# Two halves of the shared expert's gate and up products computed during routing, the first in chunks inside TensorE's waits

## The chip, the cores and the metric

One Trainium2 chip, of which the kernel uses one core. The metric is the device time of one execution in microseconds (us), from the first to the last instruction with what lies around it. TensorE is called PE, VectorE DVE, ScalarE ACT, GpSimd POOL and SyncE SP, as in the profile; L1384 is line 1384 of the kernel.

## The reference, cut to what matters

Two layers over 272 tokens (16 meta tokens and 256 of the sequence) of width 1024, all in 32-bit floats. Each layer is a mixer, a layer norm, and a mixture of experts: 64 routed experts, of which each token takes 8, and one shared expert that every token takes.

```
scores = sigmoid(h @ w_router); biased = scores + router_bias
# group-limited top 8 of 64 -> gates
act    = silu(h @ w_gate[e]) * (h @ w_up[e]);  routed += gate * (act @ w_down[e])
shared = (silu(h @ sh_gate) * (h @ sh_up)) @ sh_down       # sh_gate, sh_up: 1024 x 256
h      = layer_norm(ALPHA * h + routed + shared)
```

The shared expert's gate and up products together have 512 output columns. Turned over (weights standing still, 272 or 256 tokens streaming), these are four **halves** of 128 rows each: j = 0 and 1 are the gate, j = 2 and 3 the up product. Each half is a sum over 8 chunks of the width, one product (a call of `pe.matmul`) per chunk. A product of 32-bit floats shows as two MATMUL records in the trace, so a half is 16 records.

## The kernel before, in words

The engines run their own instruction lists and meet through semaphores. A stage is a block; at the end of a block all engines meet before the next block begins.

**Routing** (`norm_and_route`, one block per layer). It normalises the mixer's output (`hN`), computes the router's logits and picks experts on DVE in a long chain of small instructions. PE does short pieces between: transposes of the rows for the table in device memory (`turn_rows`, L1587), counts of tokens by expert (`rank_ps`, L1597), a transpose of the selection and the gates (`both_ps`, L1603), the broadcast of two units' places (`spread_unit`, L1421 and L1422), and two products that sort the experts by load (L1612, L1616 to L1618). Between them PE waits for DVE and ACT, and there it multiplies the identity with a constant (`stay_busy(n)`, L1570: n products of 128 rows and 256 columns into bank 4, whose result nobody reads). After the sort, PE waits for the shared gate and up weights (`gu_ready`) and computes as many halves as `halves_ahead(layer)` says: one, j = 0, into bank 6. ACT then takes its SiLU (`shared_silu`, L1393), and with that the block ends. The queue SP issues, in this block, the loads of the shared weights (in layer 1; in layer 0 they are asked for earlier) and, once the order of the experts is known (`ordered`), the load of the fifth expert (L1239 the gate and up matrix, L1258 the down matrix). POOL writes the rows to device memory and issues the first two gathers of rows (L1470).

**Experts** (`experts`, one block per layer). The 64 experts are processed in 27 units of two or four experts (units 2, 7, 12, 17 and 26 have four). Six slots hold expert weights, 3 MB each; SP refills a slot as soon as PE has done with its matrices, by semaphores that PE raises after half of the gate and up products (`gu_low`), after all of them (`gu`) and after the down products (`dn`). For unit i PE runs the gate and up products (L1893), turns the next unit's gathered rows over (`turn`, L1872), combines the unit before (L1911 or L1913), and runs the down products (L1948) into banks `y0b` and `y1b` (banks 4 and 5). ACT and DVE copy these banks out (`ye0`, `ye1`; L2032 and L2116).

After the down products of unit 2 (`SHARED_UNIT`) PE computes the halves of the shared expert that routing left over, j = 1 to 3, with j = 1 in bank 7 and j = 2 and 3 in banks 4 and 5. Before j = 2 it waits for both copies of the down products:

```
for j in range(ahead, 2 * FC):
    if j == FC:
        pe.wait_ge(ye0, i + 1)
        pe.wait_ge(ye1, i + 1)
    shared_half(pe, mem, ex, hN, sh_ps[j], j)
```

Then the slot with the shared gate and up weights (`SHARED_SLOT`) is given to an expert. The first two instructions of the experts block on PE are `turn(0)` and `broadcast(2)`.

Of the kernel before, what the change touches and what calls it, by code (L numbers as in the profile page):

```python
# [25 lines left out]
DC = D // P  # L26
# [1259 lines left out]
def shared_weights(mem):  # L1286
    ring = mem["dense"]
    return ring[:, 0], ring[:, 1].rearrange("p c n -> p (c n)")[:, 0:FC * D].rearrange("p (c n) -> p c n", c=FC)
# [83 lines left out]
def halves_ahead(layer):  # L1372


    return 1


def shared_half(pe, mem, ex, hN, bank, j, cs=range(DC)):


    q, m = divmod(j, FC)
    W, w_gu = hN.shape[-1], shared_weights(mem)[0]
    for c in cs:
        mm = pe.matmul(bank[:, 0:W], w_gu[:, c, q * FF + m * P:q * FF + (m + 1) * P], hN[:, c, :],  # L1384
                       start=(c == 0), stop=(c == DC - 1))
    if cs[-1] == DC - 1:
        mm.then_inc(ex["sh_gu"], 1)
# [28 lines left out]
def spread_unit(pe, mem, ex, i, banks, W):  # L1416


    pe.wait_ge(ex["unit_selected"], i + 1)
    selw, pg = ex["selw"][:, i % AHEAD, :], mem["pg"]  # L1420
    pe.matmul(banks[0][:, 0:W], selw[0:E], pg[0:E, 0:W], start=True, stop=True)  # L1421
    pe.matmul(banks[1][:, 0:W], selw[E:], pg[E:, 0:W], start=True, stop=True).then_inc(ex["rows_broadcast"], 1)  # L1422
# [53 lines left out]
def norm_and_route(nc, k, mem, layer, ex):  # L1476
# [4 lines left out]
    hN, ident, pg, ones, ln, eps = mem["hT"][:, :, first:], mem["ident"], mem["pg"], mem["ones"], mem["ln_par"], mem["eps"]  # L1481
    with ExitStack() as inner:
# [5 lines left out]
        sh_ps = [bank[b] for b in (6, 4, 5, 3)]  # L1488
# [22 lines left out]
        key_off, number, ranks, twice, extras = (sort[:, a:b] for a, b in (  # L1511
            (0, 1), (1, 2), (2, 2 + E), (2 + E, 2 + E + P), (2 + E + P, 2 + 2 * E + P)))
        ahead, warm = halves_ahead(layer), sb("warm", [1, 1])
        loaded, gu_ready = mem["router_loaded"], mem["shared_gate_up_ready"]
        meaned, centred, squared, sq_summed, sd_ready, rooted, scaled, out = (sem(n) for n in (
            "meaned", "centred", "squared", "sq_summed", "deviation", "rooted", "scaled", "normed"))
# [10 lines left out]
        with nc.Block(no_gpsimd_drain=True) as block:  # L1527

            @block.sync
            def _(sp):  # L1530
                if layer > 0:
                    load_shared_gate_up(sp, k, mem, layer)
                load_shared_down(sp, k, mem, layer)
                sp.wait_ge(asked, 1)
                sp.wait_ge(ordered, 1)
                load_expert(sp, k, mem, layer, FIXED)
# [16 lines left out]
            @block.tensor  # L1553
            def _(pe):
                pe.wait_ge(loaded, 48 * (layer + 1))
                for c in range(DC):
                    mm = pe.matmul(bias_ps[0:E, 0:1], wr[:, c, :], shift(c), start=(c == 0), stop=(c == DC - 1))
                mm.then_inc(biased, 1)
                for c in range(DC):
                    pe.wait_ge(squared, c + 1)  # L1560
                    mm = pe.matmul(sqs[:, 0:W], ones[:], sq[:, c, :], start=(c == 0), stop=(c == DC - 1))
                mm.then_inc(sq_summed, 1)
                pe.wait_ge(weighed, 1)
                for c in range(DC):
                    pe.matmul(lg_ps[0:E, 0:W], wg[:, c, :], hN[:, c, :], start=(c == 0), stop=(c == DC - 1)).then_inc(logits, 1)

                def stay_busy(n):

                    for _ in range(n):
                        pe.matmul(bank[4][:, 0:2 * P], ident[:], steady, start=True, stop=True)  # L1570

                stay_busy(2)
                pe.wait_ge(scored, 1)
                for tt, (t0, n) in enumerate(tiles):
                    mm = pe.transpose(sc_ps[0:n, tt * E:(tt + 1) * E], lgT[:, t0:t0 + n], ident[0:E, 0:E])
                mm.then_inc(score_turned, 1)

                def turn_rows(i):
                    half, tt = divmod(i, NT)
                    t0, n = tiles[tt]  # L1580
                    pe.wait_ge(out, 4 * half + 4)
                    if i == 3:
                        pe.wait_ge(bias_in, 1)
                    elif i >= 4:
                        pe.wait_ge(rows_c, i - 3)
                    for c in range(4):
                        mm = pe.transpose(row_ps[i][0:n, c * P:(c + 1) * P], hN[:, 4 * half + c, t0:t0 + n], ident[:])  # L1587
                    mm.then_inc(rows_t, 1)

                for i in range(2 * NT):  # L1590
                    if i == NT:
                        stay_busy(1)
                    turn_rows(i)
                stay_busy(2)
                pe.wait_ge(selected, 1)
                for tt, (t0, n) in enumerate(tiles):
                    mm = pe.matmul(rank_ps[0:E, t0:W], sel[0:n, tt, :], after[0:n, tt, t0:W],  # L1597
                                   start=(tt == 0), stop=(tt == NT - 1))
                mm.then_inc(ranked, 1)
                pe.wait_ge(gated, 1)  # L1600
                pe.wait_ge(rows_c, 3)
                for tt, (t0, n) in enumerate(tiles):
                    mm = pe.transpose(both_ps[:, t0:t0 + n], sg2[0:n, tt].rearrange("p q e -> p (q e)"), ident[0:n, 0:n])  # L1603
                mm.then_inc(ranked, 1)
                stay_busy(2)
                pe.wait_ge(placed, 2)
                pe.wait_ge(rows_c, 2 * NT)
                for i in range(2):
                    spread_unit(pe, mem, ex, i, spread_ps[i], W)
                pe.wait_ge(mem["expert_consts"], 16 * len(EXPERT_CONSTS))  # L1610
                pe.wait_ge(keyed, 1)
                pe.matmul(key_ps[0:E, 0:E], ones[0:E, 0:E], keys[:], start=True, stop=True).then_inc(spread, 1)  # L1612
                stay_busy(1)
                pe.wait_ge(masked, 1)
                pe.wait_ge(placed_by, 2)
                pe.matmul(sort_ps[:, 2 * E:2 * E + 1], twice, rank[:], start=True, stop=True)  # L1616
                pe.matmul(sort_ps[0:1, 0:E], number, at_rank[:], start=True, stop=True)
                pe.matmul(sort_ps[0:1, E:2 * E], cm[:], at_rank[:], start=True, stop=True).then_inc(sorted_, 1)  # L1618
                pe.wait_ge(gu_ready, 32 * (layer + 1))
                for j in range(ahead):  # L1620
                    shared_half(pe, mem, ex, hN, sh_ps[j], j)

            @block.scalar
# [134 lines left out]
def experts(nc, k, mem, layer, ex, out=None):  # L1758
# [11 lines left out]
    with ExitStack() as inner:  # L1770
# [18 lines left out]


        sh_ps, ahead = (None, bank[7], y0b, y1b), halves_ahead(layer)

        spread_to = lambda i: (y0b, y1b) if i < AHEAD else (t0b, t1b)
# [1248 lines left out]
```

## Time and profile before

| | us |
|---|---|
| median of 3 runs | 1540.65 |
| lowest and highest run | 1538.27, 1550.08 |
| the profiled execution, its own time | 1538.58 |
| its span, first to last instruction | 1536.8 |
| PE busy (share of the span) | 1441.6 (94%) |
| DVE busy | 643.1 (42%) |
| ACT busy | 342.2 (22%) |
| hardware_dynamic DMA queue | 481.75 MB, 79.2% of 16 engines' span |
| read from device memory | 508.85 MB |

The page cuts the span into 40 slices of 38.4 us. Layer 0's routing lies around 380 to 405 us and its experts from there to about 890 us; layer 1's routing lies at 1016 to 1042 us and its experts from there to the end. In the slices of the experts the mean busy share of the 16 DMA engines is shown as 9 (90% or more) and the rate as 417 to 426 GB/s; PE is shown as 9 in nearly all of them. A busy PE here is also one that streams 32-bit floats, so PE's busy time alone doesn't say which of the two is the bound.

### The profile page before, as it was taken

To read this page: it belongs to the slowest core of one execution; us is meant where nothing else is said; L and a number is where in the kernel's file an instruction comes from. 1 tells how busy PE (TensorE), PEld (TensorE's weight loads), DVE (VectorE), ACT (ScalarE), POOL (GpSimd) and SP (SyncE) were. 2 spreads that over 40 slices of the span, in tenths; PEclk is the share of its full clock that TensorE was granted. 3 is DMA by queue.
4 is the path that set the end of the run, shared out by engine and by line. 5 is a ranking of instruction groups with operands and counts; after the bars stand their busy time and mean duration, and the time that the engine had idled before them with its cause. 6 is when DMAs were issued, how large, how long until landed. Compare 5 with 4: busy or idle time off the path is not lost. (4 is left out here: it accounts for less than half of the span.)

```text
span 1536.8 us, 24364 instructions
## 1 busy us (share of the span) xinstructions
PE 1441.6 (94%) x9446; PEld 851.0 (55%) x9446; DVE 643.1 (42%) x1451; ACT 342.2 (22%) x714; POOL 249.2 (16%) x331
## 2 busy tenths in 40 slices
PE   8999998999999999896999989999999989979996
PEld 6888768887455545352545467864543433424442
DVE  2766558532533434241433359053233333414334
ACT  3756454310410111110111030141011111101111
POOL 5789625300100000000000000011000000000000
PEclk9999999899999999998999979999999989989998
DMA  8669562058599999999999973499999999999994
GB/s 284 219 189 234 179 167 64 2 215 334 226 417 424 422 419 425 424 422 422 421 424 422 409 287 123 179 387 372 419 424 421 423 424 422 426 421 423 422 422 177
DMA packets 105680, 512.38 MB, mean 333 GB/s; under 512 B 36932, under 2 KB 42116, under 8 KB 68444
## 3 DMA queue, kind: packets, MB, share of 16 engines
q1 hardware_dynamic: 95740, 481.75, 79.2%
q0 software_dynamic: 9824, 29.05, 5.1%
q8 instruction: 78, 1.28, 0.3%
q14 instruction: 38, 0.31, 0.1%
HBM read 508.85 MB, written 17.10 MB: 342 GB/s over the span
## 5 line engine op out<-in xcount | busy, mean ns | idle before, releaser
L1893 PE MATMUL banks<-upper,e_xgT 128*64 128x512 f32 (+1 forms) x880 | 195.5, 611 | 1.8 <-DMA upper<-in_moe_gate_up 1.2
L2102 DVE TENSOR_TENSOR e_ac<-e_sl,banks 128x256 f32<-128x256 f32 x54 | 22.8, 421 | 406.2 <-ACT e_sl L2020 406.2
L366 PE MATMUL banks<-hT,dense_ring 128*128 128x272 f32 x768 | 183.3, 397 | 4.9 <-DMA dense_ring<-in_w_in 4.9
L1470 POOL DMA_INDIRECT x_xg<-rows_dram,x_idx x54 | 53.5, 991 | 823.7 <-DVE x_idx L1462 803.3
L1893 PE MATMUL banks<-dense_ring,e_xgT 128*64 128x512 f32 (+1 forms) x288 | 136.1, 628 | 34.7 <-issue 34.7
L366 PEld LDWEIGHTS banks<-hT,dense_ring 128*128 128x128 f32 x768 | 146.1, 192 | 38.4 <-DMA dense_ring<-in_w_in 5.2
L1893 PE MATMUL banks<-experts,e_xgT 128*64 128x512 f32 (+1 forms) x720 | 160.4, 608 | 1.5 <-DMA experts<-in_moe_gate_up 1.2
L2020 ACT ACTIVATE e_sl<-banks 128x256 f32<-128x256 f32 x54 | 20.7, 384 | 491.6 <-PE banks L1893 491.6
L1893 PEld LDWEIGHTS banks<-upper,e_xgT 128*64 128x64 f32 (+1 forms) x880 | 65.0, 131 | 89.5 <-issue 89.5
L1913 PE MATMUL banks<-x_sg,route_consts 128*128 128x272 f32 x432 | 104.4, 393 | 0.5 <-DVE acc L2089 0.5
L1911 PE MATMUL banks<-route_consts,x_sg 128*128 128x512 f32 x216 | 97.6, 594 | 0.8 <-DVE acc L2086 0.8
L1893 PEld LDWEIGHTS banks<-dense_ring,e_xgT 128*64 128x64 f32 (+1 forms) x288 | 37.9, 133 | 103.1 <-issue 103.1
L1893 PEld LDWEIGHTS banks<-experts,e_xgT 128*64 128x64 f32 (+1 forms) x720 | 53.1, 131 | 75.0 <-issue 75.0
L2069 DVE TENSOR_TENSOR acc<-acc,banks 128x272 f32<-128x272 f32 x208 | 89.5, 438 | 6.4 <-PE banks L1913 3.4
L2116 DVE COPY route_consts<-banks 128x512 f32<-128x512 f32 x54 | 37.4, 692 | 127.4 <-PE banks L1948 127.4
L1913 PEld LDWEIGHTS banks<-x_sg,route_consts 128*128 128x128 f32 x432 | 79.9, 190 | 17.4 <-issue 1.7
L1948 PE MATMUL banks<-experts,e_aT 128*64 128x512 f32 (+1 forms) x360 | 80.2, 596 | 5.1 <-DVE acc L2074 4.8
L1948 PE MATMUL banks<-dense_ring,e_aT 128*64 128x512 f32 (+1 forms) x304 | 80.0, 595 | 3.6 <-DVE acc L2074 3.0
L1948 PE MATMUL banks<-upper,e_aT 128*64 128x512 f32 (+1 forms) x360 | 80.2, 596 | 1.2 <-DVE acc L2069 1.2
L2074 DVE TENSOR_TENSOR acc<-acc,banks 128x512 f32<-128x512 f32 x100 | 68.7, 688 | 22.4 <-PE banks L1911 20.0
L1893 PE MATMUL banks<-x_gate_up,e_xgT 128*64 128x512 f32 (+1 forms) x160 | 75.1, 625 | 0.0
L1872 PEld LDWEIGHTS banks<-ident,x_xg 128*128 128x128 f32 x432 | 46.2, 141 | 46.1 <-issue 43.7
(452 smaller groups left out, 2061.2 us busy)
## 6 DMA issues: line engine op xcount, KB each, us to landing
upper<-in_moe_gate_up SPq DMA_DIRECT2D x45, 2048.0 KB, 26.9
experts<-in_moe_gate_up SPq DMA_DIRECT2D x36, 2048.0 KB, 27.7
upper<-in_moe_down SPq DMA_DIRECT2D x43, 1024.0 KB, 26.2
experts<-in_moe_down SPq DMA_DIRECT2D x43, 1024.0 KB, 26.5
dense_ring<-in_moe_down SPq DMA_DIRECT2D x38, 1024.0 KB, 25.7
dense_ring<-in_moe_gate_up SPq DMA_DIRECT2D x18, 2048.0 KB, 19.8
dense_ring<-in_w_in SPq DMA_DIRECT2D x47, 512.0 KB, 5.4
upper<-in_moe_gate_up SPq DMA_DIRECT2D x20, 1024.0 KB, 14.5
```

The lines of the kernel that those rows point to most:

```text
L366: mm = pe.matmul(ps[g % 4][:, 0:T], slot[:, n % SLOTS_IN, c, :], hT[:, c, :], start=(c == 0), stop=(c == DC - 1))
L1470: pool.indirect_dma_start(out=ex["xg"][:, i % 2, :], out_offset=None, in_=mem["rows_dram"], in_offset=bass.IndirectOffsetOnAxis(ap=ex["idx ...
L1872: mm = pe.transpose((t0b, t1b)[c // 4][:, (c % 4) * P:(c % 4 + 1) * P], xg[:, i % 2, c * P:(c + 1) * P], ident[:])
L1893: mm = pe.matmul(gub[e * n:(e + 1) * n, :], xgT[:, i % 2, c, e * n:(e + 1) * n], gate_up_weights(mem, j)[:, c, :], start=(c == 0), stop=(c ...
L1911: pe.matmul(cb[m][:], sg[:, i % 4, tokens], ys[:, columns], start=True, stop=True).then_inc(cmm, 1)
L1913: pe.matmul(cb[m % 4][:, 0:W], ys[:, m * P:(m + 1) * P], sg[:, i % 4, :], start=True, stop=True).then_inc(cmm, 1)
L1948: mm = pe.matmul(yb[e * n:(e + 1) * n, :], aT[:, f, e * n:(e + 1) * n], down_weights(mem, j)[:, f, h * BLOCK:(h + 1) * BLOCK], start=(f == ...
L2020: act.activation(sl[:], gub[:, 0:FF], ACT.Silu).then_inc(sil, 1)
L2069: dve.tensor_tensor(acc[:, m, 0:W], acc[:, m, 0:W], cb[m % 4][:, 0:W], ALU.add).then_inc(addd, 1)
L2074: dve.tensor_tensor(total[:, tile, columns], total[:, tile, columns], cb[m][:], ALU.add).then_inc(addd, 1)
L2102: dve.tensor_tensor(ac[:], sl[:], gub[:, FF:], ALU.mult).then_inc(mul, 1)
L2116: dve.tensor_copy(ys[:, BLOCK:], y1b[:]).then_inc(ye1, 1)
```

## The change

`halves_ahead` returns 2. Half j = 0 is computed in chunks that stand in four places of PE's list in routing. In layer 0 these are 2, 2 and 1 chunks where identity products stood, and 3 after the sort; in layer 1 the first place keeps its identity products, and the others are 2 and 1 chunks, and 5 after the sort. Half j = 1 follows whole after them, in bank 4. The wait for the shared weights (`gu_ready`) and one for the normalised rows (`out`) stand ahead of each set of chunks. In the experts block `ahead` is 2 as well: after unit 2 only j = 2 and 3 are left, ACT's SiLU of m = 1 moves to routing, and the wait for `ye0` and `ye1` now stands ahead of the first half that is left. Of the eight identity products that `stay_busy` issues in each layer's list, layer 0 keeps three (2 and 1), layer 1 five.

```diff
 def halves_ahead(layer):
-    return 1
+    return 2
...
-                stay_busy(2)
+
+                def shared_chunks(cs):
+                    pe.wait_ge(gu_ready, 32 * (layer + 1))
+                    pe.wait_ge(out, DC)
+                    shared_half(pe, mem, ex, hN, sh_ps[0], 0, cs)
+
+                if layer == 0:
+                    shared_chunks(range(0, 2))
+                else:
+                    stay_busy(2)
                 pe.wait_ge(selected, 1)
...
                 mm.then_inc(ranked, 1)
-                stay_busy(2)
+                in_waits = 2 if layer == 0 else 0
+                shared_chunks(range(in_waits, in_waits + 2))
                 pe.wait_ge(placed, 2)
...
                 pe.matmul(key_ps[0:E, 0:E], ones[0:E, 0:E], keys[:], start=True, stop=True).then_inc(spread, 1)
-                stay_busy(1)
+                shared_chunks(range(in_waits + 2, in_waits + 3))
                 pe.wait_ge(masked, 1)
...
-                pe.wait_ge(gu_ready, 32 * (layer + 1))
-                for j in range(ahead):
+                shared_chunks(range(in_waits + 3, DC))
+                for j in range(1, ahead):
                     shared_half(pe, mem, ex, hN, sh_ps[j], j)
```

## Rows read from the trace of the kernel before

**Rows 1.** Busy by stretch: PE, PEld, DVE, ACT, POOL; PEclk, DMA share, GB/s.

```profile
411.00:415.00 4.00, 4.00 (x22) 1.65 (x19) 0.00 (x0) 0.38 (x1) 0.00 (x0) 1.00 0.95 372
415.00:500.00 85.00, 83.74 (x445) 46.09 (x444) 30.25 (x74) 10.11 (x23) 3.95 (x4) 1.00 1.01 421
...
1051.00:1508.00 457.00, 431.72 (x2066) 179.77 (x2062) 148.81 (x304) 56.89 (x129) 23.64 (x24) 0.98 1.01 421
```

**Rows 2.** Timeline of PE in the experts: start, us, instruction, idle before and releaser.

```profile
720.65 1.03 PE L1893 MATMUL banks<-dense_ring,e_xgT 128*32 128x512 f32 x1 [11.56 <-issue]
...
874.36 3.64 PE L1893 MATMUL banks<-upper,e_xgT 128*32 128x512 f32 x32 [1.21 <-DMA upper<-in_moe_gate_up]
...
1509.53 3.64 PE L1893 MATMUL banks<-experts,e_xgT 128*32 128x512 f32 x32 [1.18 <-DMA experts<-in_moe_gate_up]
```

**Rows 3.** Timeline of routing's end and unit 0, layer 0: PE, ACT.

```profile
394.71 1.13 PE L1597 MATMUL banks<-route_consts,r_sel_gates 128*64 128x272 f32 x6 [0.35 <-DVE r_sel_gates L1714]
...
396.82 1.13 PE L1570 MATMUL banks<-route_consts,ident 128*128 128x256 f32 x4
...
397.88 0.18 PEld L1421 LDWEIGHTS banks<-places_gates,x_selw 64*128 64x128 f32 x1 [0.33 <-DVE places_gates L1727]
...
404.64 0.40 ACT L1393 ACTIVATE shared_act<-banks 128x272 f32<-128x272 f32 x1 [3.84 <-PE banks L1384]
...
405.55 1.07 PE L1872 MATMUL banks<-ident,x_xg 128*128 128x128 f32 x8 [0.94 <-PEq L1527]
```

**Rows 4.** The same timeline in layer 1.

```profile
1033.74 1.03 PE L1570 MATMUL banks<-route_consts,ident 128*128 128x256 f32 x4
...
1037.54 3.72 PE L1384 MATMUL banks<-hT,dense_ring 128*128 128x256 f32 x16
...
1041.29 0.38 ACT L1393 ACTIVATE shared_act<-banks 128x256 f32<-128x256 f32 x1 [3.63 <-PE banks L1384]
...
1043.23 1.09 PE L1872 MATMUL banks<-ident,x_xg 128*128 128x128 f32 x8 [1.97 <-DMA x_xg<-rows_dram,x_idx]
```

**Rows 5.** Timeline after unit 2: PE and DVE, layer 0; PE, layer 1.

```profile
453.44 11.27 PE L1384 MATMUL banks<-hT,dense_ring 128*128 128x272 f32 x48
453.56 0.69 DVE L2116 COPY route_consts<-banks 128x512 f32<-128x512 f32 x1 [2.02 <-PE banks L1948]
...
1091.15 10.63 PE L1384 MATMUL banks<-hT,dense_ring 128*128 128x256 f32 x48
```

**Rows 6.** SP's queue, layer 0: issues by time; landing of the one at 403.95.

```profile
403.95 0.36 SPq L1258 DMA_DIRECT2D dense_ring<-in_moe_down  x1
411.32 4.27 SPq L1246 DMA_DIRECT2D upper<-in_moe_gate_up  x4
...
DMA to landing us min/median/max: 10.4/10.4/10.4
```

**Rows 7.** SP's queue, layer 1: issues by time; landing of the one at 1040.45.

```profile
1040.45 0.36 SPq L1258 DMA_DIRECT2D dense_ring<-in_moe_down  x1
1049.04 4.28 SPq L1246 DMA_DIRECT2D experts<-in_moe_gate_up  x4
...
DMA to landing us min/median/max: 10.8/10.8/10.8
```

**Rows 8.** SP's queue: the shared weights of layer 1; landing of both loads.

```profile
1016.97 5.41 SPq L1276 DMA_DIRECT2D dense_ring<-in_sh_up  x1
...
DMA to landing us min/median/max: 13.0/14.3/15.5
```

**Rows 9.** Chain: PE's start behind DVE's copy; four-expert units without and after a wait.

```profile
1044.36 0.70 DVE e_xgT L2055
1045.06 0.14 issue
...
1174.63 7.00 PE banks L1893 x64
...
1262.80 9.82 PE banks L1893 x64
```

## The prediction

> **What bounds the kernel now.** I first read the busy time by stretch. From 415 us on, and in layer 1 from 1051 to 1508 us, the 16 DMA engines are busy all the time (share 1.01) and move 421 GB/s, while PE is busy too but not quite (431.72 of 457.00 us) [rows 1]. Then the timeline of PE inside the experts, to see who waits for whom. PE catches up with the weights at some of the four-expert units and then stands for up to 11.56 us, and the last unit of either layer waits for its weights (1.21 and 1.18 us) [rows 2]. So each experts stage lasts from the first refill of a slot until the last weights have landed, and what counts is whether the stream of weights has holes. PE's time inside it is worth something only where PE is late with freeing a slot while the stream has run dry. The third view is the timeline of routing and SP's queue, because the stream starts from an almost empty state there: the DMA engines have the fifth expert to move and nothing else until PE is half through unit 0.
>
> **Chunks in place of identity products.** Removed: five identity products in layer 0 and three in layer 1, added as many chunks. Both are 128 rows by 128 weights; an identity product streams 256 columns, a chunk 272 in layer 0 and 256 in layer 1. Three halves, 24 products, take 11.27 us in layer 0 and 10.63 us in layer 1 [rows 5], so a chunk costs 0.47 or 0.44 us; two identity products in the same place show 1.13 us with the tail of the last one [rows 3], the same but for 16 columns (0.03 us each). The idle time behind them covers this: PE waits 0.35 us for the selection, and the weight load of the first broadcast waits 0.33 us for the places [rows 3]. I cost it at nothing in both layers; without that cover it would be 5 x 0.03 = 0.15 us. The two semaphores that stand ahead of the chunks are long raised in layer 0. The wait for `out` is covered by the transposes, which already waited for it.
>
> **The wait for the shared weights in layer 1** stands new ahead of the chunks at 1033.74 us [rows 4]. The later of the two loads is issued at 1016.97 and takes 15.5 us, so it lands at 1032.5 [rows 8], 1.2 us ahead of PE. Behind it on PE are queued both broadcasts, the keys and the sort, and for those wait ACT's copies, DVE's places, POOL's gathers and SP's fifth expert. Price today: nothing; later than 1033.7 it costs one for one.
>
> **The end of routing.** After the sort PE has 3 + 8 = 11 products in layer 0 and 5 + 8 = 13 in layer 1, where it had 8. ACT's SiLU still follows the last one, for j = 1 instead of j = 0, and costs the same. In layer 0 that is 3 x 0.47 = 1.4 us more. Nothing covers it: PE's `turn(0)` at 405.55 was released by the meeting of the engines (PEq), 0.51 us after the end of the SiLU at 405.04 [rows 3]. In layer 1 it is 5 x 0.44 = 2.2 us. There the SiLU ended at 1041.67, PE could have gone on at 1042.2, and it waited for the gathered rows until 1043.23 [rows 4], so 1.05 us are covered and 1.15 are not. Sum at the start of unit 0: +1.4 and +1.15 us on PE.
>
> **What that does to the stream.** The first refill after the fifth expert is asked for at 411.32 in layer 0 and 1049.04 in layer 1, when PE is half through unit 0 [rows 6, 7]. It now comes 1.4 and 1.15 us later. What is the stream doing then? The fifth expert's down matrix lands at 403.95 + 10.4 = 414.35, and in layer 1 at 1040.45 + 10.8 = 1051.25 [rows 6, 7]; so it still runs 3.0 and 2.2 us after the next issue, partly because the two share the engines. Bounds: if the tail is long enough, the stream has no hole and the delay costs 0; if not, it costs all 2.55 us. The row of 411 to 415 us is nearest to the question: at 372 GB/s in place of 421 the stream already lacks 4 x 49 / 421 = 0.47 us there [rows 1]. The tail is nearly used up, so I take about two thirds: 0.9 us in layer 0 and 0.7 in layer 1, **+1.6 us** together. Every microsecond of hole moves the last landing by itself, since the engines are full from then on.
>
> **After unit 2.** Half j = 1 is gone: 8 x 0.47 = 3.8 us in layer 0, 8 x 0.44 = 3.5 us in layer 1. What is late next is the pair of copies. They ran under j = 1. Now j = 2 stands first and waits for DVE's copy, which starts 0.12 us after the halves and takes 0.69 [rows 5]; with 0.14 us for the signal, as between a DVE copy and PE elsewhere [rows 9], PE stands 0.95 us. PE gains 2.8 and 2.6 us net. Against its late start it is then 1.4 us early in both layers. Where does this go? Slots come free earlier, but the stream is full [rows 1]; the next four-expert unit with a wait just waits longer [rows 2]. Worth nothing.
>
> **Sum.** Against the profiled execution: 1538.58 + 1.6 = 1540.2 us. The four executions shown are 1538.27, 1538.58, 1540.65 and 1550.08; their middle is 1539.6, one microsecond above the profiled one. I forecast 1539.6 + 1.6 = **1541.2 us**. A measurement of this kernel can tell about 1%, 15 us, from no change, so this is no change by that measure.
>
> **Rival 1, the gain comes through.** If the stream were full only because slots come free just in time, PE's path would count: +1.4 - 2.8 in layer 0 and +1.15 - 2.6 in layer 1, -2.9 us, 1536.7 us. For it: PE is busy for 94% of its time, and the final waits are only 1.2 us. Against it: there are final waits at all, and 11.56 us in the middle. Chance 0.17.
>
> **Rival 2, nothing arrives.** The tail of the fifth expert covers both delays, and the gain is swallowed as well: 1539.6 us. The 3.0 and 2.2 us of overlap speak for it, the 372 GB/s against it. Chance 0.15.
>
> **Rival 3, slower: the shared weights of layer 1 come late.** Loads of the same kind show 13.0 and 15.5 us to land [rows 8]. It decides from 16.7 us on. At 20 us PE would stand for 3.3 us ahead of the broadcasts, the fifth expert would be asked for as much later while the stream is empty, and the time would be 1541.2 + 3.3 = 1544.5. It is fixed by what was queued ahead of it, and that doesn't change. Chance 0.06.
>
> **Rival 4, slower: one more fall of PE's clock.** After a long wait a four-expert unit's gate and up products take 9.82 us instead of 7.00 [rows 9]. If waits grow from place to place, one more such fall could come where PE has no slack, in the last third of a layer: +2.8 us, 1544.0. Against it: every wait that the change adds is under 1 us, and behind those of 0.94 and 1.97 us in routing the products ran at their usual length [rows 3, 4]. The Trainium skill (TensorE: Matmul & The Clock Gate, section HAM oscillation) says that a wait for data between bursts of products can send the clock back to half; the long waits of this trace agree, and by that rule alone the longer waits at four-expert units would cost more. Chance 0.05.
>
> **That it doesn't do what it says** would show as chunks pushed out of the waits, 0.15 us at most by the sizes above; it is inside the forecast.
>
> **How the numbers follow.** Forecast 0.57, rivals 0.17, 0.15, 0.06, 0.05. The forecast's own range is 1539.6 to 1543.2: from no hole on the middle of the executions to a full hole of 2.55 us on their median, 1540.65. For 8 in 10 I go down to 1536.6, which takes in most of rival 1, and up to 1546.5, which takes in rivals 3 and 4 and an execution or two of the slower kind (one of four lay 10 us up). None of the cases reaches 15 us to either side; what is left is scatter and causes that I don't see: faster 0.02, same 0.95, slower 0.03.
>
> **What the changed kernel's profile would show.** L1384 as x4, x4 and x2 records in layer 0's waits, then x22 after the sort; in layer 1 x4, x2 and x26. `turn(0)` 1.4 us later after the sort in layer 0, and no wait for the gathered rows in layer 1. A DMA share well under 0.95 for a microsecond around the first refill. After unit 2, x32 records behind a wait of about 0.95 us on DVE's copy. Longer waits of PE at the units where it waits today, and the last units still waiting for their weights. I am wrong if the last units stop waiting for weights, if the stream shows no hole, or if layer 1's chunks stand behind a wait for their weights.

## The result, and the profile after

Three sets of 21, 12 and 12 executions of the changed kernel have medians of 1548.53, 1543.99 and 1541.82 us. The first is the result: 1.0037 of the kernel before, interval 1.0019 to 1.0055, so 5.7 us more (2.9 to 8.5), within 1%. On the median of before that was given, 1540.65, this is 1546.35 us: outside the forecast's own range, which ended at 1543.2, and 0.15 us inside the wider one, which ended at 1546.5. The second and third sets are the unchanged repeats `e1` and `e11` below: 1.0011 [0.9982, 1.0041] and 1.0001 [0.9982, 1.0021]. Over all 45 executions the mean is 1545.7; over 134 of before it is 1541.9. The difference is 3.8 us with a standard error of 0.8. Against the executions of before taken beside each set, the means differ by 5.7, 2.4 and 0.2 us, which is more scatter between sets than that error allows for.

The profiled execution took 1548.53 us, 9.95 more than that of before, with a span of 1546.7. It is not typical, as will be seen. The page first: PE's busy time and the bytes.

```profile
span 1546.7 us, 24339 instructions
...
PE 1443.3 (93%) x9430; PEld 850.9 (55%) x9430; DVE 645.5 (42%) x1451; ACT 342.5 (22%) x714; POOL 250.1 (16%) x331
...
q1 hardware_dynamic: 95740, 481.75, 78.8%
```

The same work: PE is busy 1.7 us longer over the whole kernel and the queue moves the same 481.75 MB, in a span that is 9.9 us longer. The time is in waits of the stream of weights. Where the stream runs it runs as before [rows 1]; but in layer 0's unit 0 it stands (busy by stretch, columns as in [rows 1]):

```profile
411.00:415.00 4.00, 4.00 (x16) 2.35 (x18) 1.21 (x3) 0.97 (x2) 0.00 (x0) 0.50 0.77 322
415.00:416.00 1.00, 1.00 (x6) 0.33 (x4) 0.56 (x3) 0.00 (x0) 0.00 (x0) 0.50 0.08 25
416.00:417.00 1.00, 1.00 (x6) 0.27 (x4) 0.00 (x0) 0.00 (x0) 0.56 (x1) 0.85 0.00 0
417.00:418.00 1.00, 1.00 (x8) 0.29 (x6) 0.00 (x0) 0.00 (x0) 0.43 (x1) 1.00 0.00 0
...
440.00:870.00 430.00, 408.18 (x2126) 206.21 (x2125) 159.10 (x389) 52.81 (x119) 22.80 (x23) 0.98 1.01 422
```

From 415 to 418 us almost nothing is moved, where before had 421 GB/s (the last three columns are the granted clock, the DMA share and GB/s). PE's granted clock is at 0.50, the lower of its two levels (1.2 GHz), from 411 to 416 us, and at 1.00 again from 417. PE's timeline says why the stream stands:

```profile
393.99 1.08 PE L1384 MATMUL banks<-hT,dense_ring 128*128 128x272 f32 x4
395.38 1.13 PE L1606 MATMUL banks<-route_consts,r_sel_gates 128*64 128x272 f32 x6 [0.31 <-DVE r_sel_gates L1724]
...
397.50 1.19 PE L1384 MATMUL banks<-hT,dense_ring 128*128 128x272 f32 x4
...
399.98 0.72 PE L1384 MATMUL banks<-hT,dense_ring 128*128 128x272 f32 x2
...
401.39 5.31 PE L1384 MATMUL banks<-hT,dense_ring 128*128 128x272 f32 x22
410.84 1.97 PE L1882 MATMUL banks<-ident,x_xg 128*128 128x128 f32 x8 [4.14 <-DMA x_xg<-rows_dram,x_idx]
...
413.95 8.24 PE L1903 MATMUL banks<-upper,e_xgT 128*64 128x512 f32 x32
...
462.01 7.57 PE L1384 MATMUL banks<-hT,dense_ring 128*128 128x272 f32 x32 [0.90 <-DVE route_consts L2126]
...
877.10 8.75 PE L1903 MATMUL banks<-upper,e_xgT 128*32 128x512 f32 x64 [2.32 <-issue]
...
1043.66 1.03 PE L1384 MATMUL banks<-hT,dense_ring 128*128 128x256 f32 x4
...
1047.46 5.88 PE L1384 MATMUL banks<-hT,dense_ring 128*128 128x256 f32 x26
1054.27 1.07 PE L1882 MATMUL banks<-ident,x_xg 128*128 128x128 f32 x8 [0.93 <-PEq L1527]
...
1519.40 3.64 PE L1903 MATMUL banks<-experts,e_xgT 128*32 128x512 f32 x32 [0.48 <-DMA experts<-in_moe_gate_up]
```

The chunks sit in the waits as x4, x4 and x2 records, 1.08, 1.19 and 0.72 us; the identity products in the last two places show 1.13 [rows 3] and 0.70. After the sort come x22 and x26 records. But then PE stands 4.14 us for gathered rows, `turn(0)` runs at half clock (1.97 us for the 1.07 of [rows 3]), and so do the first of the gate and up products: 32 records take 8.24 us, 7.09 in `e1` below, and the refill is asked for when PE is half through them. The gather is POOL's, and SP loads the fifth expert beside it (timelines of POOL, then of SP):

```profile
397.22 0.51 POOL L1546 DMA_DIRECT2D rows_dram<-r_rows_tail  x1 [0.30 <-ACT r_rows_tail L1660]
402.64 1.09 POOL L1470 DMA_INDIRECT x_xg<-rows_dram,x_idx  x1 [4.91 <-DMA rows_dram<-r_rows_tail]
```

```profile
403.51 0.37 SPq L1239 DMA_DIRECT2D upper<-in_moe_gate_up  x1
404.68 0.36 SPq L1258 DMA_DIRECT2D dense_ring<-in_moe_down  x1
418.94 4.29 SPq L1246 DMA_DIRECT2D upper<-in_moe_gate_up  x4
...
1049.22 0.36 SPq L1239 DMA_DIRECT2D x_gate_up<-in_moe_gate_up  x1
...
1060.05 4.28 SPq L1246 DMA_DIRECT2D experts<-in_moe_gate_up  x4
```

POOL wrote the last rows at 397.22 and waited for them to land; its gather follows at 402.64. In before, POOL's timeline has it waiting for the indices alone:

```profile
400.73 1.09 POOL L1470 DMA_INDIRECT x_xg<-rows_dram,x_idx  x1 [3.68 <-DVE x_idx L1462]
```

There the first gather went out 2.05 us ahead of SP's load at 402.78; here it is 0.87 us ahead. It landed 8.2 us after its issue, in before 3.6. So two things may be in the 5.7 us: the later end of PE's products, which was predicted, and a late gather, which was not.

**The yardstick of what follows.** Call F the issue of the fifth expert (L1239) and R that of the first refill (L1246). "Lost" is the time that the stream lacks in the 25 us after F: 25 x (1 - rate / 421.5), with the mean rate of that stretch and the full rate between 421 and 422 [rows 1]. It leaves out how late F itself is. "Rest" is the time from R to the first product of the next mixer (layer 0) or to the end of the span (layer 1). From all 14 profiles:

| kernel profiled | R - F, 0 | lost, 0 | rest, 0 | R - F, 1 | lost, 1 | rest, 1 |
|---|---|---|---|---|---|---|
| before | 8.54 | 2.16 | 483.06 | 9.73 | 2.52 | 487.76 |
| before, again (`e4`) | 8.54 | 2.05 | 482.83 | 8.70 | 1.45 | 487.75 |
| before, asked 2 (`e9`) | 8.63 | 2.22 | 483.90 | 9.07 | 1.87 | 487.92 |
| changed, again (`e1`) | 9.91 | 2.82 | 483.29 | 10.83 | 3.71 | 488.79 |
| changed, asked 2 (`e10`) | 9.92 | 2.82 | 482.31 | 10.65 | 3.17 | 487.27 |
| changed, third (`e11`) | 9.91 | 2.94 | 482.55 | 10.52 | 3.23 | 488.17 |
| changed, late gather in layer 0 | 15.43 | 7.92 | 483.29 | 10.83 | 3.23 | 486.65 |
| chunks only (`e2`) | 9.27 | 2.58 | 483.46 | 8.58 | 1.45 | 487.95 |
| halves only (`e3`) | 12.21 | 5.13 | 482.43 | 12.12 | 4.36 | 486.54 |
| gain only (`e5`), late in layer 1 | 8.54 | 2.16 | 483.58 | 16.39 | 9.16 | 487.09 |
| before, late (`e6`) | 15.94 | 8.45 | 482.91 | 9.35 | 2.88 | 488.30 |
| changed, late (`e7`) | 17.22 | 9.58 | 483.20 | 10.82 | 3.35 | 487.29 |
| chunks, busy (`e8`), late in layer 0 | 15.23 | 8.63 | 484.15 | 8.86 | 1.57 | 487.80 |
| before, landed (`e12`) | 9.33 | 3.77 | 482.80 | 10.62 | 4.18 | 487.11 |

"Rest" is 482.3 to 484.2 and 486.5 to 488.8 whatever the kernel. What a kernel does to the time is in "lost" and ahead of F. Ahead of F there is scatter in what no edit touches: routing of layer 0 starts at 377.6 to 380.1 us (384.2 in e7; its first DVE instruction), and from the first product of the next mixer to the start of layer 1's routing it is 120.9 to 124.4 us. So the time of one profiled execution says little, and its stretches say more.

### The profile page after: what moved, and what is told of

Same layout as the page of the kernel before. It is cut to its first block and busy times, and to the rows that moved or that the text cites. A ratio compares the mean times of both kernels' runs of the same rounds, so it can differ in the third digit from the quotient of the medians.

```text
span 1546.7 us, 24339 instructions
## 1 busy us (share of the span) xinstructions
PE 1443.3 (93%) x9430; PEld 850.9 (55%) x9430; DVE 645.5 (42%) x1451; ACT 342.5 (22%) x714; POOL 250.1 (16%) x331
## 3 DMA queue, kind: packets, MB, share of 16 engines
q1 hardware_dynamic: 95740, 481.75, 78.8%
```

## The experiments

Each gives its ratio to the kernel before with the 95% interval. The theory was that the delay at the first refill is all that counts, the gain after unit 2 nothing, and that the late gather is an accident of single executions; the main rival, that the gain or the chunks move the time.

**e1 and e4, both kernels again.** No edit.

> The changed kernel once more, for its profile and for how its times fall. Theory (the hole in the weights' stream): the first refill of a slot after the fifth expert sets the end of an experts stage, and it depends on PE's start on unit 0. In the profiled execution of the changed kernel layer 0's first gather was issued only 0.87 us ahead of the fifth expert's load (2.05 us before the change) and took 8.2 us to land instead of 3.6; PE stood for 4.14 us, fell to the half clock, and the stream ran dry for some 4 us. If that is one of two outcomes of a race that the change doesn't touch, this profile may show either; then a profile with a gather of under 5 us in both layers has a span of 1537 + 1 to 3 us, and one with a late gather 1545 to 1549. Ratio to before 1.002 to 1.006. Rival (the change made the late gather the rule): every profile of the changed kernel shows the gather at over 8 us in layer 0.

> The kernel before, unchanged, for a second profile. Its 21 times lie in two heaps, 13 from 1533.3 to 1542.4 and 8 from 1545.8 to 1550.1. Theory (a race for the queues that both kernels have): in the upper heap layer 0's first gather lands late, as in the changed kernel's profile; so this profile has either two early gathers and a span of 1532 to 1540, or a late one and 1544 to 1548. Rival (the heaps are something else): a span of 1544 or more with both gathers under 5 us. Ratio 1.000.

e1: 1.0011 [0.9982, 1.0041], 1543.99 us. e4: 0.999 [0.9963, 1.0016], 1539.72 us. The profile of e1 (timeline of PE, then its rates over the 25 us) has no late gather:

```profile
402.66 5.31 PE L1384 MATMUL banks<-hT,dense_ring 128*128 128x272 f32 x22
408.91 1.06 PE L1882 MATMUL banks<-ident,x_xg 128*128 128x128 f32 x8 [0.94 <-PEq L1527]
...
410.85 7.09 PE L1903 MATMUL banks<-upper,e_xgT 128*64 128x512 f32 x32 [0.22 <-DVE e_xgT L2065]
```

```profile
404.77:429.77 25.00, 23.11 (x116) 10.57 (x117) 5.27 (x15) 3.59 (x8) 2.27 (x3) 1.00 0.97 374
1043.68:1068.68 25.00, 23.10 (x116) 11.24 (x116) 5.59 (x16) 3.93 (x9) 2.98 (x3) 1.00 0.93 359
```

R comes 9.91 us after F, the predicted 1.4 later than in before (8.54), and full clock stays. The late gather is not part of the change by necessity: it costs the profiled execution 5.5 us at R. Expected for such a profile was a span of 1538 to 1540 us; it was 1543.3. Its layer 0 routing starts at 379.69 us, where that of before started at 377.64, and layer 1 adds 2.1 us for the 1.15 forecast (see below).

**e2, the chunks alone**, with one half ahead as in before:

```diff
 def halves_ahead(layer):
-    return 2
+    return 1
```

> Half j = 0 in chunks in the waits as in the changed kernel, but only one half in routing (ahead = 1), so 3 and 5 products after the sort in place of 8. Theory (hole): PE could start unit 0 2.35 us earlier in layer 0 and 1.3 in layer 1, but the gathered rows land only 1.2 us ahead of PE in layer 0 and already set the start in layer 1; so -0.3 to -1.2 us against before, ratio 0.999 to 1.000. Rival (chunks in waits cost something by themselves, by the new wait or the interrupted sum): slower than before by 1 us or more, and most of the changed kernel's +5.7 us is seen here. Rival (PE's path counts): -3.6 us, ratio 0.9976.

1.0018 [0.9992, 1.0044], 1545.63 us. Not the gain of 0.3 to 1.2 us that was expected: PE had its products done early and then waited 2.67 us for the block's end, and ran on at the lower clock (0.50 granted). SP's issue of the fifth expert is the likely holder of the block: its second load is issued until 405.13, 0.66 us ahead of PE's start (timeline of PE):

```profile
401.48 1.64 PE L1384 MATMUL banks<-hT,dense_ring 128*128 128x272 f32 x6
405.79 1.92 PE L1882 MATMUL banks<-ident,x_xg 128*128 128x128 f32 x8 [2.67 <-PEq L1527]
```

So R - F became 9.27 in layer 0, 0.7 more than in before. In layer 1 it is 8.58 with 1.45 lost, as in e4.

**e3, the second half alone**, 16 products after the sort and the identity products kept. The edit against before, `shared_chunks` being that of the change:

```diff
-    return 1
+    return 2
...
-                pe.wait_ge(gu_ready, 32 * (layer + 1))
-                for j in range(ahead):
+                shared_chunks(range(DC))
+                for j in range(1, ahead):
```

> Two halves in routing (ahead = 2), both whole after the sort; the identity products stay in the waits. 16 products after the sort in place of 8. Theory (hole): PE starts unit 0 3.8 us later in layer 0 and 3.5 - 1.05 = 2.45 in layer 1, 6.2 us together, of which the tail of the fifth expert hides at most 2: +4 to +6 us against before, ratio 1.003 to 1.004. Rival (PE's path counts, the 8 products saved after unit 2 come back): +0.9 us, ratio 1.0006.

1.0027 [1.0002, 1.0052], 1544.71 us: 4.2 us more, as expected (4 to 6), and not the 0.9 of the rival in which PE's path counts. R - F is 12.21 in layer 0 with 5.13 us lost, against 9.91 with 2.8 to 2.9 for the changed kernel. From 8.54 to 9.91 the stream loses 0.7 of 1.37 us, from there to 12.21 all of the 2.3. The tail of the fifth expert covers about half of the change's delay in layer 0 and nothing of more.

**e5, the gain alone**: before, but after unit 2 half j = 1 is only its last product. Seven eighths of that half are left out.

```diff
-                       start=(c == 0), stop=(c == DC - 1))
+                       start=(c == cs[0]), stop=(c == DC - 1))
...
-                            shared_half(pe, mem, ex, hN, sh_ps[j], j)
+                            shared_half(pe, mem, ex, hN, sh_ps[j], j, range(DC - 1, DC) if j == 1 else range(DC))
```

> The kernel before, but of half j = 1 after unit 2 only the last of its 8 products is computed in either layer (7/8 of the sum of that half is left out). So PE saves 3.3 us in layer 0 and 3.1 in layer 1 at the place where the change saves, less what then shows of the wait for the copies, and nothing is added at routing's end. Theory (the stream sets the end): the time from the first refill of a slot to the end of the stage stays at its 482.4 to 483.5 us in layer 0 and 486.5 to 488.8 us in layer 1, so nothing is gained, ratio 1.000. Rival (PE's path counts): -2.4 and -2.2 us, ratio 0.997, and both stretches shorter by that.

1.0062 [1.0030, 1.0094], 1548.83 us: nothing gained, and slower than the 1.000 expected. Its timeline of PE has the first long wait of the experts at 629.21:

```profile
629.21 1.03 PE L1893 MATMUL banks<-dense_ring,e_xgT 128*32 128x512 f32 x1 [10.87 <-issue]
...
723.69 1.03 PE L1893 MATMUL banks<-dense_ring,e_xgT 128*32 128x512 f32 x1 [11.46 <-issue]
...
1051.89 1.97 PE L1872 MATMUL banks<-ident,x_xg 128*128 128x128 f32 x8 [7.90 <-DMA x_xg<-rows_dram,x_idx]
```

In before that first wait was 6.71 us, at 625.63: 4.16 us more standing, while the second is 11.46 for 11.56 [rows 2]. "Rest" in layer 0 is 483.58. PE's gain is all swallowed there. In the changed kernel the two are 9.37 and 10.40. The last row is a late gather in layer 1, in a kernel whose instructions in routing are those of before. Its numbers are not: with most of a half left out in layer 0, layer 1 routes other values. Why this kernel is slower than before (three of its ten executions took 1555 to 1559 us) is not settled; a late gather in both layers would do it, but only one execution was profiled, and what the other values do to layer 1 was not tested.

**e6 and e7, late gathers on purpose**: in layer 0 POOL waits for the order of the experts, which SP waits for too, in before (e6) and in the changed kernel (e7).

```diff
                 pool.wait_ge(ex["xg_zero"], 1)
+                if layer == 0:
+                    pool.wait_ge(ordered, 1)
```

> The kernel before, with POOL's first gather in layer 0 held back until the order of the experts is known, so that it is issued some 0.9 us later than usual and under 1.5 us ahead of the fifth expert's load. Theory (race for the queues): the gathered rows then land over 8 us after their issue, turn(0) starts 15 us after the first write of the rows instead of 10.75, PE's clock falls, and the first refill comes some 6.9 us later: +5 to +7 us, ratio 1.0035 to 1.0045. Rival (the late landing in the changed kernel's profile had another cause): the gather lands 4 us after its issue, turn(0) comes at most 0.5 us later, and the ratio is 1.000.

> The changed kernel with the same hold on layer 0's first gather. Theory (whatever is later sets unit 0's start): if the gather lands late, the first refill comes at the same distance from the first write of the rows as in the kernel before with the hold (23.4 us), because PE's three more products end under the gather; so the change costs nothing in layer 0 and 2.1 us in layer 1: this kernel is 2 us slower than the kernel before with the hold. Rival (the products' delay adds up with the gather's): 3.5 us slower than that one.

e6: 1.0024 [0.9993, 1.0054], 1546.06 us. e7: 1.0055 [1.0034, 1.0075], 1548.81 us. The gather went out 0.86 us ahead of SP's load and landed 9.8 us later in e6, 9.9 in e7. For e6 a `turn(0)` at 15 us after the first write and 1.0035 to 1.0045 were expected; it came at 17.69 us, and the interval takes in that ratio and no change too, since before has late executions of its own to be compared with. Timelines of PE, e6 and then e7:

```profile
403.00 3.93 PE L1384 MATMUL banks<-hT,dense_ring 128*128 128x272 f32 x16
414.83 1.97 PE L1874 MATMUL banks<-ident,x_xg 128*128 128x128 f32 x8 [7.90 <-DMA x_xg<-rows_dram,x_idx]
...
417.93 7.12 PE L1895 MATMUL banks<-upper,e_xgT 128*64 128x512 f32 x32
```

```profile
407.29 5.31 PE L1384 MATMUL banks<-hT,dense_ring 128*128 128x272 f32 x22
419.22 1.97 PE L1884 MATMUL banks<-ident,x_xg 128*128 128x128 f32 x8 [6.61 <-DMA x_xg<-rows_dram,x_idx]
...
422.33 8.31 PE L1905 MATMUL banks<-upper,e_xgT 128*64 128x512 f32 x32
```

All ten executions of e6 lie between 1543.7 and 1548.3 us. Those of before without the edit fall in heaps: most from 1533 to 1543, 31% from 1545 on. So a late gather puts the kernel where the upper heap is; no execution of before out of that heap was itself profiled. Of the profiles with nothing held back, the three of 1546 us and more (the changed kernel, e5, e8) have a late gather and the six below have none, one of them at 1545.11 (e1). e7 was expected 2 us over e6, with nothing added in layer 0, or 3.5 if the delays add up; it is 2.8 by the medians. Under a late gather PE's three extra products cost nothing by themselves (`turn(0)` starts 17.69 and 17.82 us after the first write of the rows), but the clock comes back later (32 records in 8.31 for 7.12 us), and R comes 1.3 us later all the same.

**e8, chunks only, with PE kept busy** by three identity products behind the chunks, to see whether the clock of e2 is the 0.7 us:

```diff
                 shared_chunks(range(in_waits + 3, DC))
+                if layer == 0:
+                    stay_busy(3)
```

> Chunks in the waits with one half in routing (ahead = 1), and in layer 0 three identity products behind the last chunk, 6 products after the sort in place of 3. With 3, turn(0) of layer 0 started 10.21 us after the first write of the rows (SP's issue of the fifth expert holds the block's end), PE had idled 2.67 us, its clock fell to half, and the first refill came at 17.28 us, 0.76 later than before the change. Theory (the clock cost it): with PE busy, turn(0) still starts at 10.2 to 10.4, the eight turns take 1.07 us and not 1.92, and the first refill comes at 16.0 to 16.2 us. Rival (chunks in the waits cost something themselves): 17.2 us again. Ratio to before 0.999 to 1.000.

1.0027 [0.9999, 1.0055], 1543.67 us. Inconclusive: the profiled execution had a late gather of its own (0.86 us ahead, 8.4 us to land), so it says nothing on e2's clock, and what e2's 0.7 us are stays argued.

**Where an unforced late gather begins.** POOL issues the gathers once the rows that it wrote have landed. The slowest of these writes took 4.4, 4.7 and 5.2 us to land ahead of the three unforced late gathers (the changed kernel and e8 in layer 0, e5 in layer 1), and 3.6 to 3.9 us in every other layer of the 14 profiles but one: 4.7 us in layer 0 of e7, whose gather was held back anyway. So the write lands late first, the gather is then issued less than 0.9 us ahead of SP's load, and lands late in its turn. What delays the write isn't shown.

**e9 and e10, the late gather made impossible**: SP's load of the fifth expert waits until POOL has issued both of the first gathers (`asked`) instead of one, in before (e9) and in the changed kernel (e10).

```diff
-                sp.wait_ge(asked, 1)
+                sp.wait_ge(asked, 2)
```

> The kernel before, with SP waiting for both of POOL's gathers to be issued (asked at 2 in place of 1) before it asks for the fifth expert. Theory (the late landing comes when the fifth expert's load is issued under a microsecond behind the first gather): the load now always stands over 2 us behind it, so the heap of executions over 1545 us goes; where the rows are written in time the load is asked for at most 0.5 us later and the first refill comes at the same 16.5 and 15.4 us. No time over 1545, mean 2 to 3 us under the kernel before, ratio 0.998 to 0.999. Rival (the heaps have another cause): the same heaps, ratio 1.000.

> The changed kernel with the same wait. Theory: the late landings are gone here too, and what is left of the change is 1.4 us in layer 0 and 2.1 in layer 1 at the first refill: 3 to 4 us over the kernel before with the same wait (e9), no time over 1549. Rival (the change adds something else): more than 5 us over that one.

e9: 0.9992 [0.9973, 1.0012], 1539.51 us (1537.4 to 1544.3). e10: 0.9991 [0.9972, 1.0011], 1541.62 us (1534.4 to 1543.9). None of the 24 executions reaches 1545. By the shares without the edit (31% of before, 53% of the changed kernel) one would expect ten. That takes the accident out of the comparison: the change costs 2.1 us by the medians and 1.4 by the means, with a standard error of 1.0. Expected were 3 to 4, with no time over 1549 and under the 5 of the rival; the size was half of that, and the executions alone would not tell it from nothing. What e9 was expected to do, no time over 1545 and a mean 2 to 3 us under before, came out: 1540.0 for 1542.7 in the same set.

**e11, the changed kernel a third time.** No edit.

> The changed kernel a third time, for its heaps and its ratio on the same chip as the others of this call. Theory: three heaps, some 3.5 us above those of the kernel before (which has them around 1538, 1547 and 1555), ratio 1.002 to 1.004. Rival (late gathers are as frequent as not after the change): over half of the times at 1546 or more.

1.0001 [0.9982, 1.0021], 1541.82 us, with 3 of 12 executions at 1546 or more, where the first set had 13 of 21. Expected was 1.002 to 1.004, by the rival over half of the times at 1546 or more; neither came. How often the gather is late differs from run to run.

**e12, the fifth expert's load held until the first gather has landed**, in before:

```diff
                 sp.wait_ge(ordered, 1)
+                sp.wait_ge(ex["gathered"][0], 16)
```

> The kernel before, with SP waiting until the first gather's rows have landed before it asks for the fifth expert, the strict form of e9. Theory: the load is asked for at 9.7 us after the first write of the rows in place of 8.0, so the stream starts 1.7 us later in layer 0 and 3 in layer 1, but ends its fifth expert without running dry, of which I expect half back: 1 to 3 us slower than e9, and no late heap. Rival (what counts is only the first refill's time): the first refill still comes at 16.5 us and the time is that of e9.

1.0021 [1.0002, 1.0040], 1546.21 us: slower, by 6.7 us over e9 where 1 to 3 were expected. The load goes out 2.65 us later in layer 0 and 3.4 in layer 1, the block ends late, as in e2, and PE's clock falls (timeline of PE):

```profile
409.57 1.06 PE L1873 MATMUL banks<-ident,x_xg 128*128 128x128 f32 x8 [3.03 <-PEq L1527]
...
411.54 8.42 PE L1894 MATMUL banks<-upper,e_xgT 128*64 128x512 f32 x32
```

No version was clearly faster than before; e9 is the one to keep, for its lack of an upper heap, not for its median.

## Why the prediction was right, and where it wasn't

**The bound.** Right. "Each experts stage lasts from the first refill of a slot until the last weights have landed": "rest" varies by 2 us in 14 profiles with seven edits of PE's work, and the last units of the changed kernel still wait, 2.32 and 0.48 us.

**The chunks in the waits** were costed at nothing. Right: the selection's transpose follows the second set's waits as before, and F comes 8.03 us after the first write of the rows, for 7.98, both in layer 0.

**The shared weights in layer 1** (rival 3): in time. The chunks stand at 1043.66 without a wait in the changed kernel's profile.

**The end of routing.** Layer 0: predicted 1.4 us, measured 1.42 at `turn(0)` (12.17 us after the first write for 10.75) and at R, in e1, e10 and e11. Layer 1: predicted 1.15, since 1.05 us of the wait for the gathered rows would cover the rest. From the start of routing to R, before shows 32.45 and 32.41 us (the second from e4), e10 and e11 33.56, the changed kernel and e1 34.54. So 1.1 in two executions and 2.1 in two others: the cover is there only in part of them. What decides stands at the start of routing, and the change has no part in it (timelines of PE in layer 1, before and then e4):

```profile
1017.97 4.09 PE L1561 MATMUL banks<-acc,ones 128*128 128x256 f32 x16 [0.33 <-ACT acc L1631]
```

```profile
1019.23 5.41 PE L1561 MATMUL banks<-acc,ones 128*128 128x256 f32 x16 [0.33 <-ACT acc L1631]
```

In the 4 us from there PE's granted clock is 1.00 in before and 0.58 in e4. Of the other profiles e5, e6, e7, e10 and e11 are of the first kind (1.00, 4.08 or 4.09 us), the rest of the second (0.57 to 0.62, 5.2 to 5.4 us). With the slow start the first write of the rows comes 17.04 us after the start of routing for 16.05, but the first gathered rows land at 26.4 for 26.6: PE's own path is 1.0 us later and the rows are not, so the 1.05 us of cover are used up before the change adds anything. The forecast had its cover from one execution of the first kind. Why the clock falls there isn't shown. As forecast, `turn(0)` is released by the meeting of the engines (0.93 us).

**The hole in the stream.** This is the step that was off, in layer 1 and through the cover of 1.05 us: "I take about two thirds: 0.9 us in layer 0 and 0.7 in layer 1". By the table, without late gathers, layer 0 loses 2.14 us on average in before and 2.86 in the changed kernel: +0.7, near the 0.9. Layer 1 loses 1.95 and 3.34 (four profiles): +1.4, twice the 0.7. There, R - F grows from 9.17 to 10.71 and 1.4 of the 1.5 arrive. These means mix the two kinds of start. Kind by kind, before loses 2.52 and 2.88 (e6) with the fast start and the changed kernel 3.17 to 3.35 (e10, e11, e7), +0.5 to 0.6, and F itself is up to 0.3 us later; with the slow start it is 1.45 and 1.87 (e4, e9) against 3.23 and 3.71 (the changed kernel, e1), +1.8. So the layer 1 term of 0.7 holds where the cover that it assumed is there, and the term is more than twice that where it isn't. In layer 0, half of the delay arrives. Together **2.1 us where 1.6 was forecast**, inside the named bound of 2.55. The sign that was named shows: around the refill the DMA share falls to 0.79 for a microsecond in e1 (layer 0, 415 to 416 us) and to 0.37 and 0.72 in e10 (layer 1, 1052 to 1054), where the lowest of before around its own refills is 0.87 and 0.90. The pair e9 and e10 (2.1 by medians, 1.4 by means) agrees.

**After unit 2.** Right: x32 records behind 0.90 us on DVE's copy (predicted 0.95), and worth nothing. e5 shows it alone by its profile: 4.16 us more of standing at the next long wait, and "rest" as before. Rival 1 falls with it. Rival 2, that nothing arrives, falls by the holes of the table; the executions alone (e10 over e9: 1.4 with a standard error of 1.0) would not exclude it.

**What wasn't foreseen** is why the result lies above the forecast: 5.7 us measured first, 3.8 +/- 0.8 pooled, 2.1 explained. Some executions have a late gather. In the profiled one of the changed kernel it loses 5.1 us more than in e1; e6's mean of 1546.2 is 7.4 us over those 24 executions of before in its own set that lie under 1545, some 0.7 us of it from the load, which the hold makes later too. And more of the changed kernel's executions may have one: 24 of 45 are at 1545 or above, 31% of before. But that limit counts too much, since the changed kernel lies some 2 us up without any late gather (1545.11 in e1); at 1547 it is 18 of 45, 40%. A share higher by 0.09 to 0.22 times 5 to 7 us is 0.5 to 1.5 us. Whether the change raises the share at all isn't shown: the sets of the changed kernel differ among themselves as much, and nothing in it moves POOL's write or SP's load (their distance is 2.1 us in e1, as in before). The prediction read "an execution or two of the slower kind" in the four times of before, and looked no further; the row to ask for was the issue of POOL's gather against that of SP's load. That the first set still fell inside the wide range, by 0.15 us, is luck: what the prediction described accounts for 2.1 of its 5.7 us, and the allowance at the upper end was for the kinds of slowness named in rivals 3 and 4 and for scatter.

**Rival 4** had the right mechanism in the wrong place. PE's clock does fall after a wait, in routing's end, where the late gather or the block's end makes PE stand for 2.67 us and more. The Trainium skill (TensorE: Matmul & The Clock Gate, section HAM oscillation) has a wait for data between bursts send the clock to half; e6 and the profile after agree (7.90 and 4.14 us of waiting, then 1.97 us for the 1.07 of `turn(0)`).

## What to carry to other kernels

Where a stream of weights is the bound and runs dry at one place, the time is set by when the first transfer after that place is asked for; here, work moved ahead of that moment cost up to its full length, and work taken away behind it gained nothing. To size such a hole, take the mean rate over a fixed stretch from the transfer before it. In layer 0, profiles of one kernel agree within 0.2 us by it, where the times of whole executions need dozens; in layer 1 they differ by up to 1.1 us, so more than one profile is needed. A slack that is read from one execution, like the 1.05 us of cover, can be absent in the next. When the runs of a kernel fall in heaps, look among other things for two DMA issues of different queues that race, as here, and make their order certain before comparing.

## What the runs showed of the hardware

- A small indirect gather from POOL landed 3.4 to 3.7 us after its issue when SP asked for a 2 MB load 2.0 to 2.1 us later (all in layer 0), 3.9 to 5.6 us with 1.0 to 1.3 us between them (all in layer 1, where it is 3.9 with 4.7 us between them in e12), and 8.2 to 9.9 us with 0.57 to 0.87 (e5 in layer 1, e6, e7, e8, the changed kernel).
- PE's granted clock stayed full behind waits of 1.97 us [rows 4] and 2.40 us (e8 in layer 1) and stood at half behind one of 2.67 (e2). Behind 3.03 us (e12) the first eight transposes still took 1.06, and only the products after them ran long, 8.42 for 7.09 us.
- A block can end late by an engine's issue of loads, as far as times show it: in e2 and e12 PE waited 2.67 and 3.03 us for the meeting of the engines and went on 0.66 us after the issue of SP's second load in both.
- The same 16 records at the start of layer 1's routing took 4.09 us in 6 of the 14 profiles, at a granted clock of 1.00, and 5.2 to 5.4 us in the other 8, at 0.57 to 0.62.
